# Two of eight chunks of a residual update computed by GpSimd beside VectorE

## The chip, the cores and the metric

The kernel runs on one core of one Trainium2 chip. Its time is the device time of one launch in microseconds (us). The inputs are in float32.

## What is computed

The reference runs two blocks over 256 tokens of width 1024. The first block has two layers that work on the tokens and on 256 context tokens beside them, so most of its stages see 512 tokens. Each layer is a row of sublayers (gated feed-forward, a mixer of attention and short convolution, gated feed-forward), and each of them is wrapped in the same way:

```python
def pre(t, mm, i, gi):
    return rms_norm(t, g[gi]) * (1 + mm[:, :, i + 1]) + mm[:, :, i]

def post(t, y, mm, i, gi, wres):
    return t + wres * mm[:, :, i + 2] * rms_norm(y, g[gi])

h = post(h, swiglu(pre(h, m, 0, 0), ffn_wi[0], ffn_wo[0]), m, 0, 1, 0.5)
...
h = post(h, o @ w_o, m, 3, 3, 1.0)
h = post(h, swiglu(pre(h, m, 6, 4), ffn_wi[1], ffn_wo[1]), m, 6, 5, 0.5)
```

`rms_norm` divides each token by the root of its mean square over the 1024 features. So between two sublayers stands a residual update (h becomes h plus a normalised y) and, right behind it, a new norm of h. The second block (a scan, a gated linear attention and two convolved feed-forwards) has the same pairs at 256 tokens.

## The kernel before

The state `h` stays in SBUF as 8 chunks (KD) of 128 features by 512 tokens (T2) or 256 (S). The program is a list of stages. In each stage every engine has its own hand-written instruction stream, and semaphores order them: a stream waits until another engine's counter has reached a number. All engines meet in a barrier between stages. Large matmuls are done as three products of a high and a low part (`multiply`, L499 to L501); weights are split into those parts by ScalarE (L485 in feed-forwards, L2141 in the mixer) and VectorE (L490).

What the change touches is the opening of a stage at 512 tokens. It is written in `Residual` (the update that the last stage left over) and `Norm` (the norm of the new h):

- `Residual.scalar` (L1011, L1012) makes `rstd`, the inverse root of y's mean square, by a logarithm and an exponential on ScalarE, and raises `y_rstd`.
- `Residual.vector` walks over the chunks on VectorE: y times rstd (L1026), and one step behind it `update`, h plus y (L1037), which raises `h_updated`. That is 16 instructions in one stream, each of 128 partitions by 512 elements, both inputs in SBUF.
- `Norm.scalar` squares each updated chunk on ScalarE (L852, into `sq`, a tile of the arena) and raises `h_squared`.
- `Norm.tensor` sums the squares over the partitions on TensorE with a matrix of ones (L881), eight products into one PSUM bank, and raises `sum_ready` after the eighth. Such a product is issued as two instructions.
- ScalarE turns the sum into the new `rstd` (L854, L855). Then `scaled` (L887) on VectorE, `make` (L838) and the high part (L862) on ScalarE and the low part (L896) on VectorE make the input of the stage's matmuls chunk by chunk, and TensorE starts them with the first.

The order of the squares and of the sums is that of the chunks, 0 to 7, and is fixed by counters: the n-th square waits for the n-th update, the n-th sum for the n-th square.

Four stages open so at 512 tokens: `latent` of layer 0 and of layer 1 (the mixers), `ffn1(0, 1)` and `ffn1(1, 0)`. In `ffn1(0, 1)` GpSimd streams tiles of another weight (`Ada`); in the other three it has nothing to do while the stage opens. In `latent`, TensorE first has six products of L2088 that turn tables of a bias. Stages at 256 tokens use another form of the update that reads y from PSUM (L1028).

Of the kernel before, what the change touches and what calls it, by code (L numbers as in the profile page):

```python
# [27 lines left out]
ALU = mybir.AluOpType  # L28
# [5 lines left out]
KD = D // P  # L34
# [133 lines left out]
def two_blocks(nc, a, out, stop=None):  # L168
    ctx = ExitStack()
    with ctx:  # L170
# [98 lines left out]
        def col(name, i, n=1):  # L269
# [19 lines left out]
            "input_high_parts", "input_ready", "gains_ready"))  # L289
        bank_done, post_gains, y_squared, y_added, y_summed, y_rstd, y_part = (signal(n) for n in (  # L290
# [523 lines left out]
        class Norm:  # L814
# [5 lines left out]
            def __init__(self, T, scale, shift=None, scales=None, n_scales=0, post=None):  # L820
                self.T, self.scale, self.shift, self.scales, self.n_scales = T, scale, shift, scales, n_scales
                self.post = post
                self.n_s = T // S
                mem = Arena()
                self.made, self.sq = mem.take(KD, T), mem.take(KD, T)
# [15 lines left out]
            def scalar(self, act, high_of):  # L841

                T = self.T
                if self.post is None:
                    high_of(0)
                else:
                    self.post.scalar(act)
                    high_of(1)
                    for k in range(KD):

                        act.wait_ge(h_updated.sem, h_updated.at(k + 1))
                        act.activation(self.sq[:, k, :], h[:, k, 0:T], ACT.Square).then_inc(h_squared.sem, 1)  # L852
                    act.wait_ge(sum_ready.sem, sum_ready.at(1))
                    act_chain.link(act, act.activation(rstd[:, 0:T], self.sum_bank(), ACT.Ln, scale=1.0 / D, bias=eps[:, 0:1]))  # L854
                    act.activation(rstd[:, 0:T], rstd[:, 0:T], ACT.Exp, scale=-0.5).then_inc(h_squared.sem, 1)  # L855
# [20 lines left out]
            def tensor(self, pe):  # L876
                if self.post is None:
                    return
                for k in range(KD):
                    pe.wait_ge(h_squared.sem, h_squared.at(k + 1))  # L880
                    last = pe.matmul(self.sum_bank(), ones, self.sq[:, k, :], start=(k == 0), stop=(k == KD - 1))  # L881
                last.then_inc(sum_ready.sem, 1)
# [43 lines left out]

            def done(self):
                if self.post is not None:
                    h_squared.passed(KD + 1)
                    sum_ready.passed(1)  # L930
                gains.passed(self.n_scales)
                if self.n_s == 2:
                    u_made.passed(2 * KD)
                for s_ in (h_scaled, u_high, u_ready):
                    s_.passed(KD)
                if self.post is not None:
                    self.post.done()
# [17 lines left out]
        class Residual:  # L955
# [3 lines left out]
            def __init__(self, T, scale, scales=None, n_scales=0):  # L959
                self.T, self.scale, self.scales, self.n_scales = T, scale, scales, n_scales  # L960
                self.n_s = T // S
                mem = Arena()
# [58 lines left out]
            def vector(self, dve):  # L1021
                T = self.T
                dve.wait_ge(y_rstd.sem, y_rstd.at(1))
                for k in range(KD):
# [8 lines left out]
                self.update(dve, KD - 1)  # L1033

            def update(self, dve, k):
                dve.wait_ge(y_part.sem, y_part.at(k + 1))
                dve.tensor_tensor(h[:, k, 0:self.T], h[:, k, 0:self.T], self.y[:, k, :], ALU.add).then_inc(h_updated.sem, 1)  # L1037

# [5 lines left out]
            def done(self):  # L1044
                y_summed.passed(1)
                y_rstd.passed(1)
                y_part.passed(KD)
                h_updated.passed(KD)
# [390 lines left out]
        def ffn1(l, f, norm, tail, bands_of=None, ada=None, spare=None):  # L1439
# [6 lines left out]
            pairs = 4 if ada is None else 2  # L1446
            with stage() as block:
# [67 lines left out]
                def _(pool):  # L1515
                    if isinstance(norm, FirstNorm):
                        norm.gpsimd(pool)
# [464 lines left out]
        def latent(l, norm, tail):  # L1982
# [48 lines left out]

            with stage() as block:
                @block.sync
                def _(sp):
                    stream(sp, key)
                    with after(key):
                        stream(sp, out_key)

# [1773 lines left out]
```

## Time and profile before

| | us |
|---|---|
| median of 3 runs | 2752.26 (2751.23 to 2753.14) |
| the profiled execution | 2755.32 |
| its span in the trace | 2753.6 |
| TensorE busy | 2622.2 (95%) |
| VectorE busy | 1558.3 (57%) |
| ScalarE busy | 1186.4 (43%) |
| GpSimd busy | 112.5 (4%) |

The span is what the trace covers; 1.7 us of the profiled execution lie around it. Engines are named PE (matmul), PEld (TensorE's weight load, which overlaps PE), DVE (VectorE), ACT (ScalarE), POOL (GpSimd) and SP. A bracket behind an instruction says how long its engine had been idle and what released it. An instruction that starts behind another on the same engine starts some tenths before the first has ended, so a pace is read from start to start.

### The profile page before, as it was taken

The page shows a single profiled execution, that of the slowest core. Times are in us where ns is not written, and L with a number is a line of the kernel's source. Part 1 is how long each engine was busy: PE and PEld are TensorE (multiplying, and loading weights), DVE is VectorE, ACT ScalarE, POOL GpSimd, SP SyncE. Part 2 cuts the span into 40 slices and gives each one's busy share as a digit, 9 for nine tenths or more (in the row PEclk, how much of TensorE's full clock was granted, in tenths as well). Part 3 has the DMA queues.
Part 4 walks back from the last instruction along what each step waited for, and adds up shares of the span by engine and source line. Part 5 has one row for each costly group of instructions (what it writes and reads, how often), then busy time and mean ns, then how long its engine had stood idle before and what let it go on. Part 6 is the DMA issues. An engine that isn't in the chain of part 4 may idle for free. (4 is left out here: it accounts for less than half of the span.)

```text
span 2753.6 us, 38940 instructions
## 1 busy us (share of the span) xinstructions
PE 2622.2 (95%) x16089; PEld 2249.8 (82%) x16089; DVE 1558.3 (57%) x2180; ACT 1186.4 (43%) x1636; POOL 112.5 (4%) x174
## 2 busy tenths in 40 slices
PE   6999999999999998999999989989988899898999
PEld 4777786876777786888886879989977899887998
DVE  5777436455777634322336574456566676565675
ACT  4222226454422225422326454444556565453663
POOL 1111300000011000000200000000000000000000
PEclk9999999999999999999999999999999999898999
DMA  9666522212566523223423234544430454432453
GB/s 313 229 220 227 137 106 63 62 61 84 181 215 213 186 93 100 68 97 112 121 77 92 62 116 160 180 155 144 165 112 31 142 182 168 138 123 76 157 170 118
DMA packets 248076, 375.50 MB, mean 136 GB/s; under 512 B 9820, under 2 KB 188568, under 8 KB 247936
## 3 DMA queue, kind: packets, MB, share of 16 engines
q1 hardware_dynamic: 228592, 300.56, 32.8%
q0 software_dynamic: 18768, 70.85, 8.0%
q8 instruction: 103, 1.69, 0.3%
q10 hardware_dynamic: 576, 2.10, 0.2%
q14 instruction: 37, 0.30, 0.0%
HBM read 372.34 MB, written 1.16 MB: 136 GB/s over the span
## 5 line engine op out<-in xcount | busy, mean ns | idle before, releaser
L499 PE MATMUL ps<-uh,wh 128*128 128x256 f32 (+1 forms) x4128 | 1383.5, 335 | 53.8 <-DVE ul L896 32.6
L500 PE MATMUL ps<-ul,wh 128*128 128x256 f32 (+1 forms) x4128 | 1366.2, 331 | 0.0
L501 PE MATMUL ps<-uh,wl 128*128 128x256 f32 (+1 forms) x4128 | 1365.5, 331 | 0.0
L499 PEld LDWEIGHTS ps<-uh,wh 128*128 128x128 f32 x4128 | 793.0, 192 | 169.8 <-issue 54.8
L501 PEld LDWEIGHTS ps<-uh,wl 128*128 128x128 f32 x4128 | 793.1, 192 | 71.3
L500 PEld LDWEIGHTS ps<-ul,wh 128*128 128x128 f32 x4128 | 793.7, 192 | 67.4 <-issue 0.7
L490 DVE TENSOR_TENSOR wl<-ring,wh 128x2048 fp32r<-128x2048 f32 (+1 forms) x209 | 475.3, 2274 | 479.8 <-ACT wh L485 376.5
L485 ACT ACTIVATE wh<-ring 128x2048 fp32r<-128x2048 f32 x155 | 296.9, 1916 | 713.4 <-PE ps L501 709.4
L1238 DVE TENSOR_TENSOR wl<-ring,wh 128x2048 fp32r<-128x2048 f32 x66 | 151.3, 2292 | 300.3 <-ACT uh L1256 281.6
L762 DVE SCALAR_TENSOR_TENSOR arena<-arena,act_c 128x384 f32<-128x384 f32 x420 | 228.6, 614 | 86.3 <-DMA arena<-in_w_ada_dram 86.0
L1235 ACT ACTIVATE wh<-ring 128x2048 fp32r<-128x2048 f32 x66 | 126.5, 1916 | 335.4 <-PE ps L501 335.4
L1737 ACT ACTIVATE wh<-ring 128x2048 fp32r<-128x2048 f32 (+2 forms) x38 | 70.0, 1841 | 118.7 <-PE ps L501 113.2
L499 PE MATMUL ps<-wh,uh 128*128 128x256 f32 (+2 forms) x352 | 103.4, 294 | 0.0
L501 PE MATMUL ps<-wh,ul 128*128 128x256 f32 (+2 forms) x352 | 100.4, 285 | 0.0
L500 PE MATMUL ps<-wl,uh 128*128 128x256 f32 (+2 forms) x352 | 100.3, 285 | 0.0
L881 PE MATMUL ps<-arena,const 128*128 128x256 f32 (+1 forms) x144 | 65.7, 620 | 28.6 <-ACT arena L852 28.1
L881 PEld LDWEIGHTS ps<-arena,const 128*128 128x128 f32 x144 | 36.3, 263 | 57.7 <-ACT arena L852 44.4
L1927 ACT ACTIVATE arena<-ps,softs 128x512 f32<-128x512 f32 (+1 forms) x72 | 43.7, 614 | 77.7 <-DVE softs L1966 62.6
L2454 DVE SCALAR_TENSOR_TENSOR arena<-ps,cols,arena 128x255 f32<-128x255 f32 x176 | 72.6, 475 | 0.0
L499 PEld LDWEIGHTS ps<-wh,uh 128*128 128x128 f32 x352 | 68.8, 195 | 2.1 <-issue 1.7
L500 PEld LDWEIGHTS ps<-wl,uh 128*128 128x128 f32 x352 | 68.8, 195 | 1.1 <-issue 1.0
L501 PEld LDWEIGHTS ps<-wh,ul 128*128 128x128 f32 x352 | 68.8, 196 | 0.0
(367 smaller groups left out, 2200.4 us busy)
## 6 DMA issues: line engine op xcount, KB each, us to landing
ring<-in_ffn_wi_dram SPq DMA_DIRECT2D x88, 1024.0 KB, 7.5
arena<-in_w_ada_dram POOLq DMA_DIRECT2D x84, 768.0 KB, 5.1
ring<-in_ffn_w_up_dram SPq DMA_DIRECT2D x44, 1024.0 KB, 7.0
ring<-in_ffn_wo_dram SPq DMA_DIRECT2D x20, 2048.0 KB, 7.8
ring<-in_ab_w_in_dram SPq DMA_DIRECT2D x13, 2048.0 KB, 7.7
ring<-in_ffn_w_down_dram SPq DMA_DIRECT2D x10, 2048.0 KB, 7.6
ring<-in_c_w_in_dram SPq DMA_DIRECT2D x6, 2048.0 KB, 8.1
ring<-in_w_in_dram SPq DMA_DIRECT2D x20, 512.0 KB, 6.4
```

The source lines that it names most:

```text
L485: act.activation(shape_of(wh[b]), raw, ACT.Copy).then_inc(high.sem, 1)
L490: dve.tensor_tensor(shape_of(wl[b]), raw, shape_of(wh[b]), ALU.subtract).then_inc(split.sem, 1)
L499: pe.matmul(to, sh, mh, start=start and n == 0, stop=False)
L500: pe.matmul(to, sh, ml, start=False, stop=False)
L501: mm = pe.matmul(to, sl, mh, start=False, stop=stop and last)
L762: ins = dve.scalar_tensor_tensor(out=ada_folds[s], in0=ada_slot[:, kk, :], scalar=c, in1=ada_folds[s], op0=ALU.mult, op1=ALU.add)
L881: last = pe.matmul(self.sum_bank(), ones, self.sq[:, k, :], start=(k == 0), stop=(k == KD - 1))
L1235: return act.activation(wh[side(self.key, g)][:, :], self.weights(g), ACT.Copy)
L1238: return dve.tensor_tensor(wl[side(self.key, g)][:, :], self.weights(g), wh[side(self.key, g)][:, :], ALU.subtract)
L1737: act.activation(shaped(wh[side(key, g)]), raw, ACT.Copy).then_inc(high.sem, 1)
L1927: ins = act.activation(probs[:, s % 2, e, c], ps[:, 3 + e, c], ACT.Exp, bias=self.small(0, s, 4)[:, i:i + 1], accum_out=self.small(1, s, 4 ...
L2454: ins = dve.scalar_tensor_tensor(out=conv_buf[:, q, part, to], in0=ps[:, 2 * q + part, of], scalar=channel("ffn_conv_w", tap, part, g), in ...
```

## The change

In the three stages `latent(0)`, `ffn1(1, 0)` and `latent(1)`, chunks 6 and 7 of the update go to GpSimd: `share_updates` sets `post.beside` to (6, 7). `Residual.gpsimd` waits for the same `y_rstd` as VectorE and then does y times rstd and h plus y for chunk 6 and for chunk 7, with a wait of its own between the two steps. VectorE's loop ends after chunk 5. Squares and sums follow `order`, which is 0, 1, 6, 2, 3, 7, 4, 5. A square of chunk 6 or 7 waits for GpSimd's counter, the others for VectorE's. `latent` gets a stream for GpSimd, which it had not. `ffn1(0, 1)` and everything at 256 tokens keep their order.

```diff
@@ Norm
                 self.n_s = T // S
+                self.order = list(range(KD))
@@ Norm.scalar
-                    for k in range(KD):
-
-                        act.wait_ge(h_updated.sem, h_updated.at(k + 1))
+                    for k in self.order:
+
+                        self.post.updated(act, k)
                         act.activation(self.sq[:, k, :], h[:, k, 0:T], ACT.Square).then_inc(h_squared.sem, 1)
@@ Norm.tensor
-                for k in range(KD):
-                    pe.wait_ge(h_squared.sem, h_squared.at(k + 1))
-                    last = pe.matmul(self.sum_bank(), ones, self.sq[:, k, :], start=(k == 0), stop=(k == KD - 1))
+                for n, k in enumerate(self.order):
+                    pe.wait_ge(h_squared.sem, h_squared.at(n + 1))
+                    last = pe.matmul(self.sum_bank(), ones, self.sq[:, k, :], start=(n == 0), stop=(n == KD - 1))
@@ Norm
+            def share_updates(self):
+
+                if self.n_s == 2 and self.post is not None:
+                    self.post.beside = (6, 7)
+                    self.order = [0, 1, 6, 2, 3, 7, 4, 5]
+
+            def gpsimd(self, pool):
+                if self.post is not None and self.post.beside:
+                    self.post.gpsimd(pool)
@@ Residual.vector
-                for k in range(KD):
+                mine = KD - len(self.beside)
+                for k in range(mine):
...
-                self.update(dve, KD - 1)
+                self.update(dve, mine - 1)
@@ Residual
+            def gpsimd(self, pool):
+
+                pool.wait_ge(y_rstd.sem, y_rstd.at(1))
+                for n, k in enumerate(self.beside):
+                    pool.tensor_tensor(self.y[:, k, :], self.y[:, k, :], rstd[:, 0:self.T], ALU.mult).then_inc(y_part_beside.sem, 1)
+                    pool.wait_ge(y_part_beside.sem, y_part_beside.at(n + 1))
+                    pool.tensor_tensor(h[:, k, 0:self.T], h[:, k, 0:self.T], self.y[:, k, :], ALU.add).then_inc(h_updated_beside.sem, 1)
+
+            def updated(self, eng, k):
+
+                if k in self.beside:
+                    eng.wait_ge(h_updated_beside.sem, h_updated_beside.at(self.beside.index(k) + 1))
+                else:
+                    eng.wait_ge(h_updated.sem, h_updated.at(k + 1))
@@ ffn1
+            if ada is None:
+                norm.share_updates()
@@ latent
+            norm.share_updates()
```

GpSimd's stream before, between the last instructions of the first feed-forward and the next one's weight tiles (barriers and branches are rows too; L734 is a weight load of `ffn1(0, 1)`):

```order
L1824 DMA gate_bias<-in_ab_fg_bias_dram 128x16
L1825 DMA a_log<-in_ab_a_log_dram 128x32
L1447 UNCONDITIONAL_BRANCH [waits rest_loaded]
L1514 UNCONDITIONAL_BRANCH [waits barrier_Pool_Activation_PE_DVE_SP_gather]
L734 DMA arena<-in_w_ada_dram 128x4x384
```

And after the change, at the same place, where the stage `latent(0)` now lies between:

```order
L1856 DMA gate_bias<-in_ab_fg_bias_dram 128x16
L1857 DMA a_log<-in_ab_a_log_dram 128x32
L1480 UNCONDITIONAL_BRANCH [waits rest_loaded]
L2072 UNCONDITIONAL_BRANCH [waits barrier_Pool_Activation_PE_DVE_SP_gather]
L1057 ISA
L1057 TENSOR_TENSOR arena<-arena,rstd 128x512 [waits y_rstd]
L1059 TENSOR_TENSOR h<-h,arena 128x512 [waits y_part_on_gpsimd]
L1057 TENSOR_TENSOR arena<-arena,rstd 128x512
L1059 TENSOR_TENSOR h<-h,arena 128x512 [waits y_part_on_gpsimd]
L2065 UNCONDITIONAL_BRANCH
```

Four instructions on tiles have come in. The row `ISA` in front of them stands at the first of the three stages alone; the two others have only the four.

ScalarE's stream in `latent(0)` before, from the split of a weight tile to the new rstd:

```order
L2141 ACTIVATE wh_56<-ring_50 128x2048 [waits slot1_loaded]
L852 ACTIVATE arena<-h 128x512 [waits h_updated] x8
L854 ACTIVATE rstd<-ps,eps 128x512 [waits norm_sum_ready]
```

And after:

```order
L2178 ACTIVATE wh_56<-ring_50 128x2048 [waits slot1_loaded]
L854 ACTIVATE arena<-h 128x512 [waits h_updated] x2
L854 ACTIVATE arena<-h 128x512 [waits h_updated_on_gpsimd]
L854 ACTIVATE arena<-h 128x512 [waits h_updated] x2
L854 ACTIVATE arena<-h 128x512 [waits h_updated_on_gpsimd]
L854 ACTIVATE arena<-h 128x512 [waits h_updated] x2
L856 ACTIVATE rstd<-ps,eps 128x512 [waits norm_sum_ready]
```

The eight squares are the same in number; the third and the sixth now wait for GpSimd, and those behind them in the stream wait with them.

## Rows read from the trace of the kernel before

**Rows 1.** The page: span, busy time and share of each engine.

```profile
PE 2622.2 (95%) x16089; PEld 2249.8 (82%) x16089; DVE 1558.3 (57%) x2180; ACT 1186.4 (43%) x1636; POOL 112.5 (4%) x174
```

**Rows 2.** The updates' line in four windows: DVE busy, count, granted PE clock, DMA.

```profile
400.00:460.00 60.00, 5.41 (x8) 0.94 0.33 105
600.00:760.00 160.00, 5.41 (x8) 0.96 0.36 120
1000.00:1300.00 300.00, 5.41 (x8) 0.99 0.27 88
1300.00:1500.00 200.00, 5.40 (x8) 0.99 0.31 98
```

**Rows 3.** Timeline of `latent(0)`: start, duration, engine, line, [idle before <- releaser].

```profile
431.64 0.63 ACT L1012 ACTIVATE rstd<-rstd 128x512 f32<-128x512 f32 x1
...
432.38 1.29 DVE L1026 TENSOR_TENSOR arena<-arena,rstd 128x512 f32<-128x512 f32 x2 [1.04 <-ACT rstd L1012]
...
433.59 0.69 DVE L1037 TENSOR_TENSOR h<-h,arena 128x512 f32<-128x512 f32 x1
...
434.19 0.69 DVE L1026 TENSOR_TENSOR arena<-arena,rstd 128x512 f32<-128x512 f32 x1
...
435.74 0.19 PEld L881 LDWEIGHTS ps<-arena,const 128*128 128x128 f32 x1 [0.24 <-issue]
...
436.17 0.19 PEld L881 LDWEIGHTS ps<-arena,const 128*128 128x128 f32 x1 [0.24 <-issue]
...
437.20 0.69 DVE L1037 TENSOR_TENSOR h<-h,arena 128x512 f32<-128x512 f32 x1
...
437.92 0.63 ACT L852 ACTIVATE arena<-h 128x512 f32<-128x512 f32 x1 [0.57 <-DVE h L1037]
...
438.60 0.34 PEld L881 LDWEIGHTS ps<-arena,const 128*128 128x128 f32 x2 [0.52 <-ACT arena L852]
...
442.01 2.29 DVE L490 TENSOR_TENSOR wl<-ring,wh 128x2048 fp32r<-128x2048 f32 x1
...
442.81 0.19 PEld L881 LDWEIGHTS ps<-arena,const 128*128 128x128 f32 x1 [0.30 <-ACT arena L852]
...
444.24 0.69 ACT L854 ACTIVATE rstd<-ps,eps 128x512 f32<-128x512 f32 x1 [1.47 <-PE ps L881]
```

**Rows 4.** The same stage behind the sum, to its first matmul.

```profile
445.62 1.89 DVE L887 TENSOR_TENSOR arena<-h,rstd 128x512 f32<-128x512 f32 x3 [1.32 <-ACT rstd L855]
...
448.97 0.77 PE L499 MATMUL ps<-uh,wh 128*128 128x512 f32 x1 [4.77 <-DVE ul L896]
```

**Rows 5.** Timeline of `ffn1(1, 0)`: first update and the sums.

```profile
1083.11 1.29 DVE L1026 TENSOR_TENSOR arena<-arena,rstd 128x512 f32<-128x512 f32 x2 [1.05 <-ACT rstd L1012]
...
1085.72 0.50 PEld L881 LDWEIGHTS ps<-arena,const 128*128 128x128 f32 x2 [5.31 <-ACT arena L852]
...
1088.44 0.34 PEld L881 LDWEIGHTS ps<-arena,const 128*128 128x128 f32 x1 [0.52 <-ACT arena L852]
...
1089.05 0.19 PEld L881 LDWEIGHTS ps<-arena,const 128*128 128x128 f32 x1 [0.27 <-issue]
...
1093.55 0.19 PEld L881 LDWEIGHTS ps<-arena,const 128*128 128x128 f32 x1 [0.31 <-ACT arena L852]
```

**Rows 6.** GpSimd's groups with a shape: count | busy us, mean ns of one | idle.

```profile
L3439 POOL MEMSET arena<- 128x512 f32 x1 | 0.5, 545 | 0.0
...
L1833 POOL MEMSET arena<- 128x90 f32 x2 | 0.4, 193 | 0.0
```

**Rows 7.** GpSimd's first compute of the program, and DMAs that it issues (last: us to landing).

```profile
0.25 0.10 POOL L3800 MEMSET const-float32-0.0<- 128x1 f32 x1 [0.25 <-issue]
...
arena<-rpb_padded POOLq DMA_DIRECT2D x48, 64.0 KB, 6.5
```

More of the change, by code:

```diff
@@ L289, in two_blocks @@
             "input_high_parts", "input_ready", "gains_ready"))
+        h_updated_beside, y_part_beside = signal("h_updated_on_gpsimd"), signal("y_part_on_gpsimd")
         bank_done, post_gains, y_squared, y_added, y_summed, y_rstd, y_part = (signal(n) for n in (
@@ L961, in __init__ @@
                 self.n_s = T // S
+                self.beside = ()
                 mem = Arena()
@@ L1046, in done @@
                 y_rstd.passed(1)
-                y_part.passed(KD)
-                h_updated.passed(KD)
+                y_part.passed(KD - len(self.beside))
+                h_updated.passed(KD - len(self.beside))
+                for s_ in (y_part_beside, h_updated_beside):
+                    s_.passed(len(self.beside))
         def residual1(l, i, gi, weight, T=T2):
@@ L1515, in _ @@
                 def _(pool):
-                    if isinstance(norm, FirstNorm):
-                        norm.gpsimd(pool)
+                    norm.gpsimd(pool)
                     if ada is not None:
@@ L2037, in _ @@
                         stream(sp, out_key)
+                @block.gpsimd
+                def _(pool):
+                    norm.gpsimd(pool)
                 @block.tensor
```

## The prediction

> **What bounds the kernel now.** I read the totals first. TensorE is busy 95% of the span, GpSimd 4% [rows 1], so the kernel as a whole is a row of matmuls, and time is to be had only where TensorE stands still. Next I looked for where the update runs: a window table of its line shows eight updates in each of four stages, 5.41 us busy in each [rows 2]. The second of them, around 680 us, is the one that the change leaves alone. Three stages are left, so whatever the change does, it does it three times.
>
> Then I read one opening as a timeline [rows 3]. The reader is to see a relay. ScalarE has rstd ready at 432.27 (431.64 + 0.63) and VectorE starts at 432.38. It never idles until the weight split at 442.01: 16 instructions in 442.01 - 432.38 = 9.63 us, 0.60 us from start to start (433.59, 434.19). ScalarE squares a chunk when its update is done, and TensorE sums it. Take chunk 3: its update starts at 437.20, its slot of 0.60 ends at 437.80, the square runs from 437.92, and the sum's first weight load is at 438.60. So a sum begins 0.80 us behind the end of its update's slot. The last sum begins at 442.81 and the new rstd at 444.24. From there all runs to the first matmul at 448.97 [rows 4], for which TensorE has waited 4.77 us. The opening is a chain, and a shift of the last sum is a shift of the stage. The weight split at 442.01 hides in the wait for the new rstd: it ends at 444.30, VectorE is wanted again at 445.62 [rows 3, 4].
>
> A second limit lies close under the first. A sum is two passes, and where TensorE isn't waiting they follow each other by 0.43 us (435.74, 436.17) [rows 3]: 0.86 us for a sum, against 1.20 us for VectorE's two instructions for a chunk. In `latent` TensorE comes to the first sum only at 435.74.
>
> **The change, part by part.** I measure each case by when the last sum begins, against 442.81.
>
> *VectorE's part.* Four instructions leave in each stage: 4 x 0.60 = 2.40 us off its stream. If this were all, the eight sums, not VectorE, would be last. From 435.74 the eighth begins 7 x 0.86 = 6.02 us later, at 441.76, a gain of 1.05 us in each `latent`. In `ffn1(1, 0)` the third sum begins at 1088.44 and its first pass takes 0.61, since TensorE has just stood idle for 5.31 us [rows 5]. With 0.43 for the second pass and four sums more, the eighth begins at 1088.44 + 1.04 + 3.44 = 1092.92 instead of 1093.55, a gain of 0.63. The three stages give 2 x 1.05 + 0.63 = 2.7 us. This is the most that the change can bring by its own steps, half of what would count as faster. VectorE's weight split then ends earlier too and stays hidden.
>
> *GpSimd's part.* It adds four instructions in each stage, in pairs with a wait between, 12 in all. The trace has no GpSimd instruction with an input. The nearest rows are its memsets: 128x512 in 545 ns, 128x90 in 193 [rows 6], so 0.83 ns an element and 118 ns around it, and 0.43 us for 512 elements. Below: if the two inputs stream one after the other and the output beside them, 0.12 + 2 x 0.43 = 0.97 us. Above: if all three streams go in turn, 0.12 + 3 x 0.43 = 1.40. I take T = 1.2 us, the middle, as no row is nearer to either end. The Trainium skill, GPSIMD Engine Reference, section 3.1, gives 4497 ns for an add of 2048 float32 elements; by elements alone that is an estimate of 1.12 us here. No run here shows it.
>
> *Do the two run beside each other?* Every VectorE instruction of this stretch reads two SBUF tiles, and so does every new one of GpSimd. The trace shows nothing like it: GpSimd is silent in all these openings. So the cost to VectorE is bounded by nothing at all (it keeps 0.60 us) and by full turns (while GpSimd's instruction runs, VectorE stands). I work out full turns as my forecast, because that is what one shared path to the tiles would do and VectorE asks for it without a pause for 9.6 us. That is a choice between two ends, not a reading, and both ends stay in the range. The Trainium skill, SBUF — State Buffer, section "Who interferes with whom", says that a VectorE instruction with two SBUF inputs contends with a GpSimd instruction that reads SBUF, and that the shared pair of ports is an exclusive lock. By that rule the change gives the sum of the next paragraph; without contention it gives the gain of 2.7 us. No trace here can show which.
>
> *The sum with full turns.* Until GpSimd's four are done, each of them stands between two of VectorE's. VectorE's first five are y0, y1, h0, y2, h1, and all four of GpSimd's lie before the end of h1. So the slot of chunk 1's update ends at 432.38 + 5 x 0.60 + 4T = 435.38 + 4T, and its sum begins 0.80 later. Now the fixed order bites: chunks 6 and 7 are ready by then or nearly, but stand behind chunk 1, as do 2, 3, 4, 5. TensorE has six more sums to begin before the last, 6 x 0.86 = 5.16. VectorE's seven remaining instructions take 4.20 and need 0.80 behind them, so they are done before. The last sum begins at 441.34 + 4T, against 442.81: a loss of 4T - 1.47 us. With T = 1.2 that is 3.33 us. `ffn1(1, 0)` gives the same: 1083.11 + 3.00 + 4T + 0.80 + 5.16 = 1092.07 + 4T against 1093.55 [rows 5]. Three stages: 10.0 us. With T = 0.97 it is 3 x 2.41 = 7.2, with T = 1.40 it is 3 x 4.13 = 12.4. The split on VectorE ends some 2 us later, at about 446.7, and the new rstd comes at about 449.0, so it stays hidden. The profiled execution would go from 2755.32 to 2765.3; I put the shift on the median, since that is what will be compared: 2752.26 + 10.0 = 2762.3.
>
> *The waits.* ScalarE's third square waits for GpSimd, and squares 2, 3, 7, 4, 5 queue behind it, and all of TensorE's sums behind those. With free running and T = 1.2 chunk 6 is ready at 432.38 + 2.4 = 434.8 and its turn on TensorE comes only at 435.74 + 1.72 = 437.46, so the wait costs nothing; chunk 7 at 437.2 is wanted by its sum at 440.0. *The ISA row* stands ahead of the first stage's instructions. Its price is bounded below by the program's first compute on GpSimd, which starts 0.25 us in, and above by a fetch as long as a small DMA that GpSimd issues, 6.5 us to landing [rows 7]. At 6.5 from the stage's start (430.9) chunk 6 would be ready at 439.8, its sum at 440.6, and the last at 444.9: a loss of 2.1 us in that one stage in place of the gain of 1.05. With full turns it moves the forecast by less than 1 us, as VectorE works alone meanwhile. I take it at nothing and keep 3 us for it on the free side.
>
> **The rivals.**
>
> *Free running* (nobody slows): the gain of 2.7 us above, 2749.6; with a slow first call 2752.7. It decides the other way from me. For it: GpSimd is idle there and its start needs nothing but `y_rstd`. Against it: the same two-tile reads on both. The turning point for three full-turn stages to stay within no change (5.5 us, 1.8 a stage) is T = 0.83 us, below my lower bound, so the sign hangs on sharing and not on T.
>
> *Part sharing*: VectorE is stretched for as long as GpSimd needs only half of the path. The loss is then somewhere between -0.9 and +3.3 a stage; with half of 4T lost by VectorE, chunk 1's sum begins at 436.18 + 2.4 = 438.6 and the last at 443.7, +0.9 a stage, 2755.0.
>
> *GpSimd is simply slow, VectorE free*: chunk 7's update is done at 432.38 + 4T, two more sums follow its own, so the last sum begins at 434.9 + 4T. That is level with before at T = 1.98; at T = 2.5, far above my bounds, it is 2.1 us a stage and 2758.6.
>
> *GpSimd never gets a turn until VectorE is done* at 439.6: then chunk 6 is ready at 442.0, its sum begins at 442.8, five more follow: 447.1, or 4.3 us a stage, 2765.2. It is the upper end of full turns.
>
> That the change does nothing is excluded by the two streams shown: the four instructions and the two new waits are there in three stages.
>
> **How the numbers follow.** Full turns, starved GpSimd with them: 0.46. Free running: 0.28. Part sharing: 0.18. Slow GpSimd: 0.05. Something else, such as TensorE's clock rising at another moment after the wait: 0.03. About 0.2% (5.5 us) is what a measurement of this kernel can tell from no change. Slower by more: nearly all of full turns, half of slow GpSimd and a little of part sharing, 0.49. Faster by more: no case reaches 5.5 us, so 0.03 for what I don't see. Within: 0.48. The forecast's own range is 2759.4 to 2765.2. With free running, whose centre is 2749.6, the range is 2749 to 2766.
>
> **What would show it.** In the profile after: VectorE's instructions in the opening, 0.60 us apart (free) or with gaps or durations near 1.8 us while GpSimd's run (turns); GpSimd's own durations against 0.97 to 1.40; the update of chunk 1 ending at 435.4 or near 440; the first sum of chunk 6 right behind that of chunk 1; and from rstd to the last sum 10.4 us before, 9.4 (free) or 13.8 (turns). In the first stage alone, a late start of GpSimd would show the ISA row's price. If VectorE keeps its pace, the forecast is wrong in sign and the time is under 2753. If it is slower with VectorE's pace kept, T was mis-sized.

## The result, and the profile after

| | before | after |
|---|---|---|
| median | 2751.74 us (2751.22 to 2753.14, 4 runs) | 2767.37 us (2764.89 to 2769.60, 4 runs) |
| ratio, 95% interval | | 1.0052 (1.0039 to 1.0065) |
| profiled execution | 2755.32, span 2753.6 | 2764.89, span 2763.1 |

The change costs 15.6 us. The forecast was slower by 10.0 us, and the time lies 1.4 us above the range.

The totals of the profile after, which answer to [rows 1]; the two lines under them are GpSimd's new groups from the table of groups by form (count | busy us, mean ns of one | idle before):

```profile
PE 2626.5 (95%) x16089; PEld 2250.8 (81%) x16089; DVE 1563.4 (57%) x2168; ACT 1184.8 (43%) x1636; POOL 131.2 (5%) x186
```

```profile
L1059 POOL TENSOR_TENSOR h<-h,arena 128x512 f32<-128x512 f32 x6 | 9.6, 1596 | 0.5
L1057 POOL TENSOR_TENSOR arena<-arena,rstd 128x512 f32<-128x512 f32 x6 | 8.9, 1488 | 340.2 <-ACT rstd L1025 340.2
```

VectorE has 12 instructions fewer and is 5 us busier. That alone rules out that it kept its pace. The opening of `latent(0)` as a timeline (start, duration, engine, line, idle before and its releaser) answers to [rows 3]; L1040 and L1051 are now VectorE's two instructions, L854 the square, L883 the sum, L856 the new rstd:

```profile
432.10 1.27 POOL L1057 TENSOR_TENSOR arena<-arena,rstd 128x512 f32<-128x512 f32 x1 [96.13 <-ACT rstd L1025]
432.12 3.48 DVE L1040 TENSOR_TENSOR arena<-arena,rstd 128x512 f32<-128x512 f32 x2 [1.04 <-ACT rstd L1025]
...
433.45 1.60 POOL L1059 TENSOR_TENSOR h<-h,arena 128x512 f32<-128x512 f32 x1
...
435.01 1.71 POOL L1057 TENSOR_TENSOR arena<-arena,rstd 128x512 f32<-128x512 f32 x1
...
435.52 1.75 DVE L1051 TENSOR_TENSOR h<-h,arena 128x512 f32<-128x512 f32 x1
436.80 1.59 POOL L1059 TENSOR_TENSOR h<-h,arena 128x512 f32<-128x512 f32 x1
437.19 1.75 DVE L1040 TENSOR_TENSOR arena<-arena,rstd 128x512 f32<-128x512 f32 x1
...
437.98 0.30 PEld L883 LDWEIGHTS ps<-arena,const 128*128 128x128 f32 x2 [2.74 <-ACT arena L854]
...
438.87 0.68 DVE L1051 TENSOR_TENSOR h<-h,arena 128x512 f32<-128x512 f32 x1
439.47 0.68 DVE L1040 TENSOR_TENSOR arena<-arena,rstd 128x512 f32<-128x512 f32 x1
...
440.26 0.50 PEld L883 LDWEIGHTS ps<-arena,const 128*128 128x128 f32 x2 [1.98 <-ACT arena L854]
...
441.28 0.34 PEld L883 LDWEIGHTS ps<-arena,const 128*128 128x128 f32 x1 [0.52 <-ACT arena L854]
...
442.13 0.34 PEld L883 LDWEIGHTS ps<-arena,const 128*128 128x128 f32 x1 [0.52 <-issue]
...
446.30 0.19 PEld L883 LDWEIGHTS ps<-arena,const 128*128 128x128 f32 x1 [0.42 <-issue]
...
448.02 0.19 PEld L883 LDWEIGHTS ps<-arena,const 128*128 128x128 f32 x1 [0.24 <-issue]
...
449.50 0.69 ACT L856 ACTIVATE rstd<-ps,eps 128x512 f32<-128x512 f32 x1 [5.08 <-PE ps L883]
```

Two things are to be seen. First, VectorE and GpSimd start together, and from then on VectorE's first four instructions take (438.87 - 432.12) / 4 = 1.69 us each instead of 0.60. Each is held off for **1.09 us**; with GpSimd's last instruction the pace is back at 0.60 (438.87, 439.47). Second, from 440.26 TensorE's passes are 0.85 us apart (441.28, 442.13), and only from 446.30 on 0.43, as in [rows 3]. A window table shows the granted clock for the sums (columns: window, length, weight-load busy, granted clock as a share of full, DMA share, GB/s):

```profile
436.00:438.00 2.00, 0.02 (x1) 1.00 0.00 0
438.00:446.00 8.00, 2.80 (x10) 0.58 0.00 1
440.50:446.00 5.50, 2.29 (x8) 0.50 0.00 1
446.30:449.50 3.20, 1.14 (x6) 1.00 0.61 189
```

The full clock is 2.4 GHz and a share of 0.50 is 1.2 GHz. By its weight loads TensorE had stood idle for 2.74 and 1.98 us before its first two sums (by the modelled ends of its matmuls, 1.91 and 1.15). The two loads of the first sum still take 0.30 us together, those of the second 0.50, and from then on the granted clock is at the lower level. In the kernel before, no weight load of this stage's sums came after more than 0.91 us of idleness, and the granted clock was 1.00 throughout them.

`ffn1(1, 0)` answers to [rows 5]:

```profile
1094.37 0.50 PEld L883 LDWEIGHTS ps<-arena,const 128*128 128x128 f32 x2 [8.53 <-ACT arena L854]
...
1098.33 0.19 PEld L883 LDWEIGHTS ps<-arena,const 128*128 128x128 f32 x1 [0.33 <-issue]
...
1103.68 0.69 ACT L856 ACTIVATE rstd<-ps,eps 128x512 f32<-128x512 f32 x1 [2.87 <-PE ps L883]
```

Its first sum comes after 8.53 us of idleness instead of 5.31, and its passes are slow until 1098.33. In `latent(0)` the first matmul answers to [rows 4]: the wait behind the sums is 4.77 us as before, so what comes behind the last sum moved as a block.

```profile
454.24 0.77 PE L500 MATMUL ps<-uh,wh 128*128 128x512 f32 x1 [4.77 <-DVE ul L898]
```

I compare the openings of all kernels by one length: from the first ScalarE instruction of the old update's rstd (L1011 before, L1024 after) to the first of the new rstd (L854, L856). In `latent(0)` that is 444.24 - 430.92 = 13.32 us before and 449.50 - 430.66 = 18.84 after.

| opening, us | `latent(0)` | `ffn1(0, 1)` | `ffn1(1, 0)` | `latent(1)` |
|---|---|---|---|---|
| before | 13.32 | 14.04 | 13.31 | 13.32 |
| after | 18.84 | 14.23 | 16.61 | 18.67 |

The three changed stages lose 5.52 + 3.30 + 5.35 = 14.2 us. The difference of the medians is 15.6, and the interval of the ratio makes it 10.7 to 17.9. In the profiled execution the rest of the program, which the change doesn't touch, ran some 5 us shorter than in that of before (the spans differ by 9.5). That execution is the shortest of the four; the other three took 2766.5 to 2769.6.

### The profile page after: what moved, and what is told of

Read it like the earlier page. It is cut to its first block and busy times, and to the rows that moved or that the text cites. A ratio compares the mean times of both kernels' runs of the same rounds, so it can differ in the third digit from the quotient of the medians.

```text
span 2763.1 us, 38942 instructions
## 1 busy us (share of the span) xinstructions
PE 2626.5 (95%) x16089; PEld 2250.8 (81%) x16089; DVE 1563.4 (57%) x2168; ACT 1184.8 (43%) x1636; POOL 131.2 (5%) x186
## 3 DMA queue, kind: packets, MB, share of 16 engines
q8 instruction: 103, 1.69, 0.3%
## 5 line engine op out<-in xcount | busy, mean ns | idle before, releaser
L883 PE MATMUL ps<-arena,const 128*128 128x256 f32 (+1 forms) x144 | 67.6, 638 | 37.6 <-ACT arena L854 37.6
L883 PEld LDWEIGHTS ps<-arena,const 128*128 128x128 f32 x144 | 36.5, 264 | 68.7 <-ACT arena L854 52.7
```

## The experiments

The theory was: (a) the two engines take turns at the SBUF reads, (b) the fixed order then makes chunk 1's sum late and puts six more behind it, (c) TensorE's clock falls in the wait that this opens. Rivals were that GpSimd is merely slow, that the waits or the order alone cost the time, and that the low clock is harmless.

### Contention without any moved work

VectorE keeps its eight chunks in the old order. GpSimd runs the same four instructions on tiles that nobody uses, and ScalarE waits for them before the new rstd.

```diff
-                    self.post.beside = (6, 7)
-                    self.order = [0, 1, 6, 2, 3, 7, 4, 5]
+                    self.extra = "reads"
...
+                z = [gates[:, i, :] for i in range(4)]
+                if self.extra == "reads":
+                    for n in range(2):
+                        pool.tensor_tensor(z[2], z[0], z[1], ALU.mult).then_inc(y_part_beside.sem, 1)
+                        pool.wait_ge(y_part_beside.sem, y_part_beside.at(n + 1))
+                        pool.tensor_tensor(z[3], z[0], z[2], ALU.add).then_inc(h_updated_beside.sem, 1)
...
```

> VectorE keeps all eight chunks and the old order; GpSimd does four instructions of the same shape and kind on tiles that nobody uses, from the same y_rstd on, in the same three stages; only the Ln of the new rstd waits for their end. Theory (turns: VectorE stands while GpSimd's two-input instruction runs, 1.09 us each): the last sum begins 4 x 1.09 = 4.4 us later in each stage, 13.1 us in all or more if TensorE's clock falls in the longer waits, 2765 to 2771. Rival (the loss comes from waiting for GpSimd's results and from the order): VectorE keeps 0.60 us from start to start and the time stays at 2752.

Measured: 2767.87 us against 2752.07, ratio 1.0064 (1.0047 to 1.0081). The openings are 17.72, 17.70 and 17.71 us, each 4.4 longer. Its timeline in `latent(0)`:

```profile
432.09 1.27 POOL L945 TENSOR_TENSOR arena<-arena 128x512 f32<-128x512 f32 x1 [96.77 <-ACT rstd L1054]
432.11 3.48 DVE L1069 TENSOR_TENSOR arena<-arena,rstd 128x512 f32<-128x512 f32 x2 [1.05 <-ACT rstd L1054]
...
437.18 1.75 DVE L1069 TENSOR_TENSOR arena<-arena,rstd 128x512 f32<-128x512 f32 x1
438.85 0.68 DVE L1080 TENSOR_TENSOR h<-h,arena 128x512 f32<-128x512 f32 x1
```

These are the durations of the changed kernel, with no tile shared and nothing moved. The hold is the price: 4 x 1.09 = 4.36 us of the 4.4. So (a) is shown, and it comes from the instructions being there at once, whoever's tiles they work on. TensorE's clock fell here too, behind the same waits (2.74 and 1.98 us; the granted clock is 0.74 from 440.00 to 446.00), but it cost next to nothing: here the chunks come 1.20 us apart, and by the last of them TensorE is at the full clock again and waits for VectorE. The low clock costs time only where the sums still lag when the last one is due.

### Which instructions hold which

One kernel in which VectorE keeps all its chunks, with another kind of GpSimd work on unused tiles in each stage (the helper of the run before, told which kind): two inputs in `latent(0)`, memsets in `ffn1(1, 0)`, copies in `latent(1)`, two inputs beside the 256-token form in `ffn1(1, 1)`.

```diff
-                norm.share_updates()
+                norm.share_updates("writes" if f == 0 else "reads")
...
-            norm.share_updates()
+            norm.share_updates("reads" if l == 0 else "copies")
```

> A probe, read stage by stage. VectorE keeps all chunks; GpSimd works on unused tiles in four openings: latent(0) four two-input instructions of 128x512, ffn1(1, 0) four memsets of 128x1024, latent(1) four copies of 128x512 (one input each), ffn1(1, 1), a stage of 256 tokens, four two-input instructions beside VectorE's L1028 form, one of whose inputs lies in PSUM. Theory (turns at one shared reading path): latent(0) shows four VectorE starts 1.69 us apart, ffn1(1, 0) none longer than 0.60, latent(1) some longer ones by the length of a copy's reading, and in ffn1(1, 1) only the h plus y instructions, with both inputs in SBUF, are held. Rival (any access of GpSimd holds VectorE): the memsets stretch VectorE by about 1 us each too, and both kinds are held in ffn1(1, 1). Second rival (turns by instruction whatever it reads): the same.

Measured in the timelines of `ffn1(1, 0)` (memsets), `latent(1)` (copies) and `ffn1(1, 1)`:

```profile
1090.84 0.95 POOL L951 MEMSET arena<- 128x1024 f32 x1 [140.70 <-ACT rstd L1053]
1090.89 1.29 DVE L1068 TENSOR_TENSOR arena<-arena,rstd 128x512 f32<-128x512 f32 x2 [1.04 <-ACT rstd L1053]
1092.10 0.68 DVE L1079 TENSOR_TENSOR h<-h,arena 128x512 f32<-128x512 f32 x1
```

```profile
1473.89 0.61 POOL L958 COPY arena<-arena 128x512 f32<-128x512 f32 x1 [103.60 <-ACT rstd L1053]
1473.93 2.12 DVE L1068 TENSOR_TENSOR arena<-arena,rstd 128x512 f32<-128x512 f32 x2 [1.04 <-ACT rstd L1053]
...
1475.58 0.95 POOL L958 COPY arena<-arena 128x512 f32<-128x512 f32 x1
1475.98 1.09 DVE L1079 TENSOR_TENSOR h<-h,arena 128x512 f32<-128x512 f32 x1
```

```profile
1649.94 1.33 POOL L946 TENSOR_TENSOR arena<-arena 128x512 f32<-128x512 f32 x1
1650.07 0.47 DVE L1070 SCALAR_TENSOR_TENSOR arena<-ps,post_scale,rstd 128x256 f32<-128x256 f32 x1
1650.46 1.09 DVE L1079 TENSOR_TENSOR h<-h,arena 128x256 f32<-128x256 f32 x1
```

Beside memsets VectorE keeps 0.60 us a step. Beside a copy an instruction takes 1.09 us instead of 0.68, so it is held for 0.41; beside two inputs it is held for 1.09. In the last stage the instruction that reads its tile from PSUM takes its 0.47 us with GpSimd at work, and the one with both inputs in SBUF is the one that stretches, to 1.09 us where it takes 0.41 once GpSimd is done (1654.69); GpSimd's instruction had begun half a microsecond before it, so this isn't a whole hold. The hold goes with the inputs that GpSimd reads: one input 0.41, two 1.09, none nothing. That it is the time of GpSimd's reading is the plain explanation, but no run measures the reading by itself. In all pairs tried it falls only on VectorE instructions with two SBUF tiles. The time of this kernel (2763.28 us, one run) is a mixture and says nothing by itself.

### Order of completion as it really is

```diff
-                    self.order = [0, 1, 6, 2, 3, 7, 4, 5]
+                    self.order = [6, 0, 7, 1, 2, 3, 4, 5]
```

> The changed kernel with squares and sums in the order 6, 0, 7, 1, 2, 3, 4, 5, the order in which its trace shows the updates end. Theory: VectorE's stream is as in the changed kernel, 4 x 1.09 - 2.40 = 1.96 us longer than before; the sums are no longer queued behind chunk 1, so the last sum follows VectorE's end: 1.96 us a stage, 5.9 in all, 2757.6 if TensorE's clock stays up; up to 2762 if it falls in the gaps. Rival (the order does not matter, VectorE alone sets the end): the changed kernel's loss stays, 2767.

Measured: 2760.61 us against 2752.07, ratio 1.0033 (1.0021 to 1.0046); openings 15.22, 15.22 and 15.21, each +1.90. With this order the last sum simply follows VectorE's last update, so the loss is 4T less the 2.40 us that have left VectorE: 4 x 1.09 - 2.40 = 1.96. The sums in `latent(0)`:

```profile
437.67 0.34 PEld L883 LDWEIGHTS ps<-arena,const 128*128 128x128 f32 x2 [0.52 <-ACT arena L854]
...
439.88 0.30 PEld L883 LDWEIGHTS ps<-arena,const 128*128 128x128 f32 x2 [1.88 <-ACT arena L854]
```

The waits between the sums are 1.88 us and less, and behind the first the loads take the 0.30 us that two of them take at the full clock. (b) is shown: compared with this order, the order on record costs 3.6 us in `latent(0)` and 1.4 in `ffn1(1, 0)`. The 3.6 hold both the queue of sums and the low clock; the next run parts them. In `ffn1(1, 0)` of this run TensorE was at the low clock too, until 1096.60, and the opening is no longer than the others. But even the right order doesn't make the change pay.

### TensorE kept busy in the latents

The order of the change, with eight passes on constants (three matmuls ahead of the first sum and one ahead of the second, two passes each) where TensorE would wait.

```diff
+                fill = {0: 3, 1: 1} if self.keep_busy else {}
+                if self.keep_busy:
+                    pe.wait_ge(y_rstd.sem, y_rstd.at(1))
                 for n, k in enumerate(self.order):
+                    for _ in range(fill.get(n, 0)):
+                        pe.matmul(ps[:, 0, 0:T2], ones, const[:, 0:T2], start=True, stop=True)
                     pe.wait_ge(h_squared.sem, h_squared.at(n + 1))
```

> The changed kernel; in the two latent stages TensorE does three products of constants into a free bank after the bias tables and before the first sum, and one before the second, so that it does not stand idle. Theory (the 2.6 us that a latent stage loses beyond the turns are sums at the lower clock after 2.7 and 2.0 us of waiting): the sums of latent are 0.86 us apart instead of 1.7, a latent stage loses 2.9 us against before instead of 5.4, all three 9.2, about 2761 to 2762. Rival (they are queueing or something else): sums stay 1.7 us apart at first and the time stays at 2767 or grows by the products' own length.

Measured: 2762.42 us, ratio 1.0042 (1.0028 to 1.0056). The latent openings fall from 18.84 and 18.67 to 15.93 and 15.90; `ffn1(1, 0)`, without fillers, stays at 17.61. Window (PE, PEld, DVE, ACT, POOL busy, clock, DMA) and last sums in `latent(0)`:

```profile
438.00:446.00 8.00, 8.00 (x20) 3.31 (x18) 7.88 (x10) 4.16 (x7) 0.32 (x1) 1.00 0.00 1
```

```profile
445.01 0.19 PEld L889 LDWEIGHTS ps<-arena,const 128*128 128x128 f32 x1 [0.24 <-issue]
445.44 0.19 PEld L889 LDWEIGHTS ps<-arena,const 128*128 128x128 f32 x1 [0.24 <-issue]
```

The added wait for `y_rstd` holds nothing up: rstd is there at 431.92, TensorE comes to its first constants at 435.40. Same order, the sum of chunk 1 at the same place (440.18 against 440.26), more work for TensorE, and 2.9 and 2.8 us less. So (c) is shown for the latents, and turns with the fixed order alone cost +2.6 a stage: 1.9 for the holds less what left VectorE, as in the run before, and 0.7 for the queue of sums.

### One chunk instead of two

```diff
-                    self.post.beside = (6, 7)
-                    self.order = [0, 1, 6, 2, 3, 7, 4, 5]
+                    self.post.beside = (7,)
+                    self.order = [7, 0, 1, 2, 3, 4, 5, 6]
```

> The changed kernel with only chunk 7 on GpSimd, squares and sums in the order 7, 0, 1, 2, 3, 4, 5, 6. Theory: each GpSimd instruction holds VectorE for 1.09 us and each chunk takes 1.20 off its stream, so one chunk costs 2 x 1.09 - 1.20 = 0.98 us a stage, half of what two cost in the order of completion (1.90): 2.9 us in all, about 2755. Rival (there is a fixed price of sharing, or the first chunk is free because VectorE has slack): near 1.9 or near 0 a stage.

Measured: 2756.10 us against 2752.44, ratio 1.0014 (1.0005 to 1.0024); openings 14.29, 14.92 and 14.30. Two holds in place of two instructions are 2 x 1.09 - 2 x 0.60 = 0.98; the latents show 0.97 and 0.98. `ffn1(1, 0)` shows 1.61, with TensorE's clock low there in addition. (The profiled execution, 2760.62 us, was the longest of the ten.) The loss goes by the instruction, for one chunk and for two: an instruction that leaves VectorE saves 0.60 us and holds it for 1.09.

### The change in the feed-forward alone, and in the latents alone

The first edit, in `latent`, leaves the sharing to `ffn1(1, 0)`; the second, in `ffn1`, leaves it to the latents.

```diff
-            norm.share_updates()
```

```diff
-            if ada is None:
-                norm.share_updates()
```

> The changed kernel, but only ffn1(1, 0) shares its update; both latent stages are as before. Theory: that stage alone loses what it lost in the changed kernel, 3.3 us, and the others nothing: 2755.4. Rival (sharing also costs something outside the openings, since the changed kernel's median lost 1 us more than its three openings show): more than 4.5 us, 2756.5 or above.

> The changed kernel, but only the two latent stages share their update; ffn1(1, 0) is as before. Theory: they lose 5.4 us each, of which 2.9 are turns and 2.5 sums at the lower clock: 10.8 us, 2763.2. Together with the run of ffn1(1, 0) alone (4.3 us in the median) this must give the changed kernel's 15.6. Rival (there is a price outside the openings): the two do not add up.

Measured: feed-forward alone 2756.78 us, ratio 1.0015 (1.0006 to 1.0025), its opening 18.06 (+4.75), the latents at 13.32. Latents alone 2761.72 us against 2752.68, ratio 1.0033 (1.0019 to 1.0047), openings 15.91 and 17.37, the unshared `ffn1(1, 0)` 14.32. In latents alone the same code came out in two ways in one execution; `latent(0)` and then `latent(1)`:

```profile
444.18 0.30 PEld L883 LDWEIGHTS ps<-arena,const 128*128 128x128 f32 x2 [1.98 <-ACT arena L854]
444.72 0.19 PEld L883 LDWEIGHTS ps<-arena,const 128*128 128x128 f32 x1 [0.24 <-ACT arena L854]
...
1479.74 0.50 PEld L883 LDWEIGHTS ps<-arena,const 128*128 128x128 f32 x2 [1.98 <-ACT arena L854]
1480.76 0.34 PEld L883 LDWEIGHTS ps<-arena,const 128*128 128x128 f32 x1 [0.52 <-ACT arena L854]
...
1483.04 0.19 PEld L883 LDWEIGHTS ps<-arena,const 128*128 128x128 f32 x1 [0.24 <-issue]
```

The same waits (2.7 and 1.98 us), and the clock stays up in the first (granted 1.00 from 444.18 to 450.50) and falls in the second (0.79 from 1479.74 to 1487.00). What decides between the two, no run here shows. `latent(0)` is a second measurement of what the turns cost without the clock: +2.59. The expectation of 5.4 us for each latent was not met (2.59 and 4.05). And the unshared `ffn1(1, 0)` of this run, in which nothing is changed, took 1.0 us more than before: after the same 5.31 us of idleness as in [rows 5] its clock stayed low until about 1097, where in [rows 5] it was up at 1089.05.

```profile
1092.68 0.33 PEld L883 LDWEIGHTS ps<-arena,const 128*128 128x128 f32 x1 [0.38 <-issue]
...
1097.43 0.19 PEld L883 LDWEIGHTS ps<-arena,const 128*128 128x128 f32 x1 [0.24 <-issue]
```

So an opening of this stage can be 1 us longer with no change at all, and a single execution of it says little about the last microsecond. The time from the sum behind the long wait to the first fast pass was 3.3 us in `latent(1)` here (1479.74 to 1483.04), 6.0 in `latent(0)` of the changed kernel (440.26 to 446.30), and 6.7 in the feed-forward-alone kernel, counted there from the first sum (1088.39 to 1095.10). The two kernels' medians add up to 4.3 + 9.0 = 13.3 us of the 15.6. By their intervals they stand for 1.7 to 6.9 and 5.2 to 12.9 us, so this neither shows nor rules out a price outside the openings.

### Is the low clock behind the last sum a cost too?

TensorE of the kernel before also falls to the low level, in the wait behind the last sum [rows 4]. Here it is kept busy there: the kernel before, with five matmuls on constants behind the last sum of each 512-token opening.

```diff
                 last.then_inc(sum_ready.sem, 1)
+                if self.n_s == 2:
+                    for _ in range(5):
+                        pe.matmul(ps[:, 0, 0:T2], ones, const[:, 0:T2], start=True, stop=True)
```

> The kernel before, with five products of constants on TensorE behind the last sum in the four openings at 512 tokens, 4.3 us of work in its wait of 4.8 us for the first input. Theory (TensorE's clock falls because it stands idle): the first matmuls of the stage run at the higher clock, 0.23 us apart instead of 0.43, for the 3 to 5 us in which they were slow; since inputs arrive only every 1.5 us, of this 0.5 to 1.5 us a stage is left, 2746 to 2750. Rival (the clock does not follow the wait, or the inputs set the pace alone): slow matmuls stay or the time stays at 2752; if the constants' products reach past the first input it is slower.

Measured: 2751.94 us against 2752.44, ratio 0.9997 (0.9987 to 1.0006). The stage's first product now takes 0.47 us where it took 0.77 [rows 4], but TensorE soon waits:

```profile
450.75 0.47 PE L499 MATMUL ps<-uh,wh 128*128 128x512 f32 x1 [0.48 <-DVE ul L899]
...
453.14 0.50 PE L499 MATMUL ps<-uh,wh 128*128 128x512 f32 x1 [0.77 <-DVE ul L899]
```

What it waits for is VectorE's low parts of the input chunks (L899), and it can't run ahead of them. The gain of 2 us or more that was expected did not come; the rival, that the inputs alone set the pace, holds. So the low clock there costs nothing that can be measured; where it was seen to cost time, TensorE's passes were themselves the chain.

### The same sharing without the hold

If only VectorE instructions with two SBUF tiles are held, half of them can be freed: ScalarE writes rstd a second time into a PSUM bank, and VectorE's products read it from there. One chunk goes to GpSimd. VectorE's stream is reordered so that GpSimd's two instructions meet mostly products.

```diff
+                if self.beside:
+                    act.activation(ps[:, 0, 0:T], rstd[:, 0:T], ACT.Exp, scale=-0.5).then_inc(y_rstd.sem, 1)
...
+                            dve.tensor_tensor(self.y[:, k, :], self.y[:, k, :], ps[:, 0, 0:T], ALU.mult).then_inc(y_part.sem, 1)
...
-                pool.wait_ge(y_rstd.sem, y_rstd.at(1))
+                pool.wait_ge(y_rstd.sem, y_rstd.at(2))
...
+                    self.post.beside = (7,)
+                    self.order = [0, 7, 1, 2, 3, 4, 5, 6]
```

> One chunk (7) on GpSimd as in the run with one chunk, but ScalarE writes rstd into a free PSUM bank first and into SBUF behind it; VectorE multiplies by the copy in PSUM, GpSimd by the one in SBUF, 0.63 us later. VectorE's order is y0 y1 h0 y2 y3 h1 h2 y4 h3 y5 h4 y6 h5 h6, so that each GpSimd instruction lies beside two multiplications with one input in SBUF; squares and sums in the order 0, 7, 1 to 6. Theory (only two inputs from SBUF on VectorE meet GpSimd's reads): the multiplications run beside GpSimd without being held, h0 waits some 0.6 us for the first GpSimd instruction, and the opening takes 0.2 us less to 0.3 us more than before, instead of the 0.97 to 1.6 more of one chunk; the time is 2752 to 2753. Rival (every VectorE instruction takes turns with GpSimd, wherever its inputs lie): the opening is 1 us or more longer, 2755 to 2757.

Measured: 2753.61 us against 2752.68, ratio 1.0003 (0.9993 to 1.0012). The latents open in 12.51 and 12.52 us, **0.8 less than before**: the sign has turned, by more than was expected. `ffn1(1, 0)` opens in 14.64, +1.33, because there TensorE's clock was low from 1087.50 to 1093.59. So the next kernel shares in the latents alone (the edit is the one of the latents-alone kernel above):

> One chunk (7) goes to GpSimd in the two latent stages alone, VectorE's products read rstd from PSUM; ffn1(1, 0) is as in the kernel before. In the run that shared in all three stages the latent openings (first ScalarE instruction of the update to the new rstd) were 12.51 and 12.52 us against 13.32 before, and ffn1(1, 0) 14.64 against 13.31. By turns held off plus the clock of TensorE: latent openings 12.5 each, ffn1(1, 0) back at 13.3, in all 1.6 us less than before, so the median 0.9990 to 1.0000 of before, a gain smaller than what a measurement can tell. Rival (the gain in the latents hangs on something that the shared ffn1(1, 0) brought along): latent openings at 13.3 and no gain. A third outcome, a latent opening of 13.5 to 15, would say that TensorE's clock at the sums varies with this form too.

Measured: 2752.05 us against 2752.46, ratio 0.9998 (0.9989 to 1.0007); openings 12.51, 13.32 and 12.51. `latent(0)`:

```profile
433.13 1.28 POOL L1067 TENSOR_TENSOR arena<-arena,rstd 128x512 f32<-128x512 f32 x1 [96.44 <-ACT rstd L1027]
...
433.81 1.15 DVE L1061 TENSOR_TENSOR h<-h,arena 128x512 f32<-128x512 f32 x1
...
434.49 1.60 POOL L1069 TENSOR_TENSOR h<-h,arena 128x512 f32<-128x512 f32 x1
...
434.88 1.27 DVE L1043 TENSOR_TENSOR arena<-arena,ps 128x512 f32<-128x512 f32 x2
```

One update (433.81) is held, for 0.47 us (1.15 instead of 0.68); the two products at 434.88 run at 0.60 us a step with GpSimd's addition beside them. VectorE's stream is shorter by two steps of 0.60 and longer by this one hold: 0.73 us. The control has the second rstd, the reads from PSUM and the same kind of order, but all eight chunks on VectorE (the edit is against the kernel just shown):

```diff
-                    self.post.beside = (7,)
-                    self.order = [0, 7, 1, 2, 3, 4, 5, 6]
+                    self.post.in_psum = True
```

> The control of the run before: the same two latent stages, the same second copy of rstd in PSUM, VectorE's products reading it from there and VectorE's instructions in the same altered order, but all eight chunks on VectorE and nothing on GpSimd. If the gain of 0.8 us an opening came from GpSimd's chunk: 16 instructions at 0.60 us as before, the last sum where it was, openings 13.3. If it came from reading rstd in PSUM or from VectorE's order: openings 12.5 or so with no sharing. Time 0.999 to 1.001 of before in either case; the openings decide.

Measured: 2753.20 us, ratio 1.0004 (0.9995 to 1.0013); openings 13.25 and 13.25 in the latents. So of the 0.81 us, 0.74 come from GpSimd's chunk and 0.07 from the form. The 0.74 agree with the 0.73 counted from the timeline. With most of the hold away, the same move shortens the opening. Two gains of 0.8 us are below what can be measured on the whole: the median of the version that shares in the latents alone is no better than before, and no version here beats it.

## Why the prediction was right in direction and short in size

*What bounds the stage.* Right. The relay of update, square, sum and rstd sets the opening in all kernels here, and the chain behind it moved as a block.

*Full turns against free running.* The choice was between two ends, and turns are what runs. Of the four rivals none holds: GpSimd starts at once and is not starved (432.10), it isn't slow (1.27 us for its first instruction), VectorE doesn't keep its pace, and it loses 1.09 us to each instruction of 1.27, far from the half that part sharing gave. The Trainium skill, SBUF — State Buffer, section "Who interferes with whom", which spoke against the change, agrees with the traces in all four kinds of pair tried: two inputs, memsets, copies, and a VectorE instruction with one tile in PSUM.

*T.* Taken as 1.2 with bounds 0.97 and 1.40; the hold is 1.09 and an unhindered GpSimd instruction lasts 1.27. The prediction had one number for both. The Trainium skill, GPSIMD Engine Reference, section 3.1, puts the 2.6 cycles an element of such an instruction down to its two inputs being read in turn; by its clock of 1.2 GHz that is an estimate of 1.11 us for 512 elements. The hold of 1.09 agrees.

*Where chunk 1's sum begins.* With the start 0.26 us earlier and T = 1.09 the working gives 435.38 - 0.26 + 4.36 = 439.48 for the end of its slot and 440.28 for its sum. The trace has 439.47 (the next instruction's start) and 440.26. The rows carried this step to the hundredth.

*Six more sums at 0.86 us.* **This is the step that failed.** The sums took 448.02 - 440.26 = 7.76 us instead of 5.16. The 0.86 was read in a stretch of [rows 3] where TensorE was never idle for long, and was applied behind waits of 2.7 and 2.0 us that the change itself makes. [rows 5] had the warning: after 5.31 us of idleness the first loads take 0.50 and 0.34 us there instead of 0.19, until 1089.05. The prediction used that for one pass and no further, and named the clock only as something else, at 0.03. From VectorE's start to the last sum it came to 13.8 us; the trace has 448.02 - 432.12 = 15.90.

The account in the openings, from the two latents with the clock up (+2.61 and +2.59):

| us | forecast | shown |
|---|---|---|
| turns with the fixed order, three stages | 10.0 | 3 x 2.6 = 7.8 |
| TensorE's clock at the sums | 0 | 2.9 + 0.7 + 2.8 = 6.4 |
| sum | 10.0 | 14.2 |

The first line is smaller than the forecast by 12 x 0.11 = 1.3 for T and the rest for the sums, whose first pair needs less than 0.86 (444.18 to 444.72 above). So the forecast was 2.2 us too high for the turns and 6.4 too low for the clock; that it missed its range by only 1.4 us is in part luck. The 2.6 is taken for `ffn1(1, 0)` too; there it isn't shown by itself, only that the excess over it varies: 0.7 in the changed kernel, 1.7 with the latents kept busy, 2.2 with the feed-forward alone. As the unshared stage varied by 1.0 too, this line of the account is argued for `ffn1(1, 0)` and shown for the latents. The remaining 1.4 us between the openings and the medians stay unassigned. Of the other kernels most show the same sign: their medians lie 0.1 to 1.4 us above what their openings say, 2.6 with the extra reads and 2.8 with the order of completion, and 0.4 below with the feed-forward alone. That may be the clock elsewhere, or only that the openings come from one execution each; these runs can't tell.

*The ISA row.* Taken at nothing, right: GpSimd's first instruction starts at 432.10, 0.02 us before VectorE's.

*The weight split.* Hidden, as said: it ended at 443.69 + 2.28 = 445.97, long before 450.89, when VectorE is wanted again.

*The range.* It ended at 2766, just above full turns with a high T. It held the bounds of the costs that were listed, and none for a TensorE that slows down. (Its lower end, 2759.4, is 2759.5 by its own sum, 2752.26 + 3 x 2.41; nothing hangs on it.)

## What to carry to other kernels

Where VectorE's stream is the chain, as here, moving part of it to GpSimd beside it lost time as long as GpSimd read while VectorE's next instructions had two SBUF tiles. Before such a move, count what leaves (0.60 us here) against what each moved instruction holds (1.09), and see whether an input can come from PSUM, which turned the sign here. Where a forecast opens a wait of a few microseconds in front of TensorE work that is itself on the chain, price that work at the low clock as well as at the full one, and put the difference into the range. An order of completion is part of the forecast, not of the intention: the durations with contention decide it.

## What the hardware showed that I had not expected

- The two engines alternate instruction by instruction when both have work ready: four GpSimd instructions, four stretched ones of VectorE, no more and no fewer, in every opening with four such instructions.
- The hold is shorter than the instruction that makes it: 1.09 of 1.27 us with two inputs, 0.41 of 0.61 with one (the difference is 0.18 and 0.20), and a memset of 128x1024 (0.95 us) holds nothing.
- GpSimd is slowed as well: in the changed kernel 1.27 us for its first instruction, which starts just ahead of VectorE's, and 1.59 to 1.71 for the three behind it.
- TensorE's clock after a wait is not a fixed price. The same waits of 2.7 and 2.0 us cost 0 in one `latent` and 1.5 to 2.9 in others (openings +2.6, +4.05, +5.35, +5.5), and the low level lasted 3.3 to 6.7 us once the sums ran.
